# Strassen's seven products for 36 of the 66 pairs of gate and up tiles, in three feed-forward layers

## The reference, cut to what matters

```python
h = rms_norm(x, g)
f = (jax.nn.silu(h @ w_gate) * (h @ w_up)) @ w_down
x = x + f            # normed first in gen 1, times 0.5 in gen 2 and 5
```

## Time and profile before

| | |
|---|---|
| median of 3 runs | 1947.0 us (1946.43 to 1948.33) |
| profiled execution | 1947.51 us, span of its instructions 1945.8 us |
| PE busy, matmuls | 1924.7 us (99% of the span), 9634 instructions |
| DVE, ACT, POOL busy | 999.6, 753.3 and 240.1 us |
| PE's share of the chain that ended last | 93% |
| HBM | 90 GB/s over the span |

### The profile page before, as it was taken

How to read it: one execution, slowest core, us unless ns; L and a number is a source line. 1 busy time by engine, 2 the same in 40 slices (tenths; PEclk the granted TensorE clock), 3 DMA queues, 4 the chain that set the end, 5 groups by cost and what they waited for, 6 DMA issues and landing times.

```text
span 1945.8 us, 23922 instructions
## 1 busy us (share of the span) xinstructions
PE 1924.7 (99%) x9634; PEld 1564.1 (80%) x9634; DVE 999.6 (51%) x1497; ACT 753.3 (39%) x1165; POOL 240.1 (12%) x240
## 2 busy tenths in 40 slices
PE   9999999999999999999999999999999999999998
PEld 7777788878888888788888888777787788888887
DVE  6677535373334345733333367887654444333335
ACT  6344534453223233432322256665543333233224
POOL 5210001201011011010100112222010011011010
PEclk9999999999999999999999999999999999999999
DMA  6222233433333323333333232222332233333323
GB/s 174 58 65 66 59 99 103 119 98 98 98 97 98 98 85 111 97 95 96 95 96 97 81 113 66 66 66 66 87 98 65 76 97 96 95 96 96 97 59 104
DMA packets 340767, 176.32 MB, mean 91 GB/s; under 512 B 6481, under 2 KB 339378, under 8 KB 340658
## 3 DMA queue, kind: packets, MB, share of 16 engines
q1 hardware_dynamic: 340658, 174.79, 30.7%
HBM read 172.67 MB, written 2.10 MB: 90 GB/s over the span
## 4 chain that ended last, share of the span: by engine, by line
PE 93%; DVE 3%; ACT 2%; DMA 1%; issue 1%; POOL 0%; SPq 0%; ACTq 0%; DVEq 0%
PE ps L1107 28%; PE ps L1109 28%; PE ps L1111 28%; PE ps L1167 1%; PE ps L1147 1%; PE ps L1156 1%; PE ps L1252 1%; PE ps L1120 1%; PE ps L1270 1%; PE ps L1130 1%; PE ps L1181 1%; PE ps L1137 0%; DVE WL L1562 0%; DMA RAW<-in_ffn_w_down 0%; ACT WH L1313 0%
## 5 line engine op out<-in xcount | busy, mean ns | idle before, releaser
L1107 PE MATMUL ps<-HH,WH 128*128 128x512 f32 x1728 | 687.8, 398 | 1.3 <-ACT HH L1323 1.3
L1111 PE MATMUL ps<-HL,WH 128*128 128x512 f32 x1728 | 673.9, 390 | 0.8 <-DVE HL L1583 0.8
L1562 DVE TENSOR_TENSOR WL<-RAW,WH 128x1024 fp32r<-128x1024 f32 (+3 forms) x335 | 400.8, 1199 | 532.5 <-ACT WH L1313 532.0
L1109 PE MATMUL ps<-HH,WL 128*128 128x512 f32 x1728 | 673.2, 390 | 0.7 <-DVE WL L1562 0.7
L1313 ACT ACTIVATE WH<-RAW 128x1024 fp32r<-128x1024 f32 (+3 forms) x335 | 337.6, 1010 | 520.2 <-PE ps L1111 516.7
L1107 PEld LDWEIGHTS ps<-HH,WH 128*128 128x128 f32 x1728 | 324.4, 188 | 78.1 <-issue 9.7
L1109 PEld LDWEIGHTS ps<-HH,WL 128*128 128x128 f32 x1728 | 324.5, 188 | 72.1 <-issue 5.5
L1111 PEld LDWEIGHTS ps<-HL,WH 128*128 128x128 f32 x1728 | 324.3, 188 | 71.5 <-DVE HL L1583 2.1
L1107 PE MATMUL ps<-GH,WH 128*128 128x512 f32 x688 | 269.2, 391 | 0.0
L1111 PE MATMUL ps<-GL,WH 128*128 128x512 f32 x688 | 267.9, 389 | 0.0
L1109 PE MATMUL ps<-GH,WL 128*128 128x512 f32 x688 | 267.8, 389 | 0.0
(11 more groups left out here) (202 smaller groups left out, 1526.8 us busy)
## 6 DMA issues: line engine op xcount, KB each, us to landing
RAW<-in_ffn_w_gu SPq DMA_DIRECT2D x88, 512.0 KB, 3.8
RAW<-in_w_in SPq DMA_DIRECT2D x67, 512.0 KB, 3.8
RAW<-in_ffn_w_down SPq DMA_DIRECT2D x32, 512.0 KB, 4.1
RAW<-in_w_gate SPq DMA_DIRECT2D x22, 512.0 KB, 3.8
RAW<-in_w_up SPq DMA_DIRECT2D x22, 512.0 KB, 3.8
RAW<-in_w_out SPq DMA_DIRECT2D x16, 512.0 KB, 4.2
RAW<-in_mem_w_kv SPq DMA_DIRECT2D x16, 512.0 KB, 4.0
RAW<-in_w_down SPq DMA_DIRECT2D x16, 512.0 KB, 3.9
```

The source lines that it names most:

```text
L1107: e.matmul(bk, wh, xh, start=k == 0, stop=False)
L1109: e.matmul(bk, wl, xh, start=False, stop=False)
L1111: last = e.matmul(bk, wh, xl, start=False, stop=k == kt - 1)
L1562: e.tensor_tensor(at.weight(n, "L"), m["RAW"][:, n % NRAW, 0:kt, :], at.weight(n, "H").bitcast(F32), ALU.subtract).then_inc(*sg.inc("lo", n))
```

## The change

In each layer the first five gate and up tiles (f 0 to 4) stay as they were. From then on `PAIRS` names tiles f that are taken together with f+1: f=5 in the first third, 0, 3 and 6 in the second, 0 and 3 in the last, 6 pairs a layer. The other tiles, f=7, then 2 and 5, and 2 and 5, stay plain. For a pair, the 256 x 1024 weights and the 1024 x 512 input are each seen as 2 x 2 blocks, and a gate (or up) matrix is seven products of one half weight tile (128 x 512) with one block of 4 chunks x 256 rows: 7 x 4 x 3 = 84 matmuls of 256 columns (`product`, L1338, L1340, L1342) where there were 48 of 512. Nothing else of the matmuls changes.

What it adds:

- DVE forms four sums of weight blocks per matrix (`combine_weights`, L1847) from the two RAW tiles; each is then split like a weight.
- During f 0 to 3 DVE makes the normalised input, chunk by chunk (`normal`, L1854, x2 a tile), POOL forms four sums of its blocks (`mix`, L2281 to L2286), ACT and DVE split them into NH and NL (`mix_split`, L1553, L1860). During the up tile of f=4 the normalised chunks take the place of HH and HL (`place`, L1558, L1866). The later plain tiles so need neither `normed` nor `gate_r`: silu reads PSUM (`gate_plain`, L1565).
- The seven products go into five banks. The sixth is added on top of the third's bank when ACT has copied that (L1570, event s1), the seventh on top of the second's when DVE has read that (`sum_two`, L1883 and L1886, event c22). DVE adds the partial results in 256-column instructions (L1873, L1883, L1886, L1891, L1909, and L1900 for up); POOL multiplies gate by up (`gate_mixed`, L2294).
- Masks for the mixer are written by POOL during the down tiles of gen 2, since NH and NL lie over their place.

The core of the diff:

```diff
+PAIRS = ((5,), (0, 3, 6), (0, 3))
+LOOK = 8
+MIXED = (("b", 2), ("c", 0), ("a", "11"), ("e", 1), ("d", 3), ("a", "21"), ("c", "22"))
...
+    def weigh_pair(self, key, name, c0):
+        n, r = len(self.weights), len(self.raws)
+        self.raws += [(name, 0, KD, c0 + P), (name, 0, KD, c0)]
+        self.weights += [("sum", key, 2), ("sum", key, 1), ("half", r + 1, 0), ("sum", key, 3), ("half", r, 1), ("half", r + 1, 1),
+                         ("sum", key, 4)]
...
+        self.spent += [r] * 4 + [r + 1] * 2 + [r + 2]
+        self.raw_done[r] = (("lo", n + 4), ("comb", (key, 3)))
+        self.raw_done[r + 1] = (("lo", n + 2), ("lo", n + 5), ("comb", (key, 4)))
...
     def split_to(self, n):
...
+            self.step("split", i, self.hfree)
             self.n_split += 1
...
+            while self.n_dma < min(len(known.raws), known.spent[i] + NRAW):
                 self.dma()
+            for w, need in zip(known.weights[i + 1:i + 1 + LOOK], known.needs[i + 1:i + 1 + LOOK]):
+                if w[0] == "sum" and need < self.n_dma:
+                    self.combine_to(w[1], max(w[2], self.combined.get(w[1], 0)))
...
+    def product(gen, key, i, n):
...
+        elif i == 5:
+            g.wait_ge(*sg.at("gate_act", ("s1", key)))
+        else:
+            g.wait_ge(*sg.at("part_sum", ("c22", key)))
...
+    def combine_weights(key, j):
...
+        g.wait_ge(*sg.at(f"d_raw{rb % NRAW}", rb))
+        g.wait_ge(*sg.at(f"d_raw{ra % NRAW}", ra))
```

More of the change, by code:

```diff
@@ L247, in turn, with split_tile @@
         return dst, ("td", dst)
[L249 to L250 removed]
+    def split_tile(self, src, ev, buf, gen, n, also=()):
+        self.step("split_tile", src, ev, buf, gen, n, (self.gfree if buf == "G" else self.hfree) + also)
+        if also:
+            self.tiles.give(src, ("xl", (buf, gen, n)))
     def scores(self, u, i, q, k):
@@ L369, in pipeline, with normal, mix @@
             step()
-    def ffn(self, gen, gate, g0, up, u0, down, evac, third0):
-        R = None
+    def normal(self, gen, c, gcol):
+        self.tiles.take(("N", gen, c))
+        self.step("normal", gen, c, gcol + c, self.norm(gen))
+    def mix(self, gen, c, gcol):
+        if c < 4:
+            self.normal(gen, c, gcol)
+            self.normal(gen, c + 4, gcol)
+            for a in range(2):
+                self.tiles.take(("mix", gen, c, a))
+            self.step("mix", gen, c)
+        if c:
+            for a in range(2):
+                self.step("mix_split", gen, c - 1, a, self.mixed_free)
+                self.tiles.give(("mix", gen, c - 1, a), ("op_lo", (gen, c - 1, a)))
@@ L375, in ffn @@
+    def ffn(self, gen, gate, g0, up, u0, down, evac, third0, gcol):
+        R, pending = None, []
         for n, (f0, nf) in enumerate(THIRDS):
@@ L398, in ffn @@
                 self.step("gate_r", key, go, R)
-                if not n == f == 0:
-                    mu, = self.mtiles([su], ("H", gen, 0), [bu])
-                self.step("gate_up", key, mu, bu)
+                if f == PLAIN - 1:
+                    self.mix(gen, f, gcol)
+                    self.tiles.give(("R", ("n", gen)), ("N", (gen, 7)), ("gr", key))
+                if f:
+                    mu, = self.mtiles([su], ("H", gen, 0), [bu], ahead=f < PLAIN - 1)
+                if f == PLAIN - 1:
+                    self.place(gen)
+                    self.ahead(len(self.weights))
+                self.step("gate_up", key, mu, bu, ("gr", key))
                 self.banks.give(bu, ("gu", key))
@@ L404, in ffn @@
                 self.tiles.give(("gt", key), ("xl", ("G", G, f)))
+                if f < PLAIN - 1:
+                    self.mix(gen, f, gcol)
+            while pending:
+                self.split_tile(*pending.pop(0))
             if n == 2:
-                self.end_norm(gen, ("pj", ("gt", (G, nf - 1))), ("gr", (G, nf - 1)))
+                self.hfree = self.mixed_free = (done,)
+                for half in range(2):
+                    self.held["L", half] = self.held["PT", half] = (done,)
             if n == 2 and gen == 5:
@@ L413, in ffn @@
                 evac(n, mt, b, mm)
-                self.split_to(len(self.weights) + NSPL)
+                if n == 2 and gen == 2:
+                    for i in LATE[mt]:
+                        self.step("consts", i, done)
+                self.ahead(len(self.weights))
             self.gfree = (mm,)
@@ L886, in second_block @@
         self.out_proj(5, "mem_w_o_2", 8, COL["ffn2_norm_2"], [step, None, lambda: turned(3), None, step])
+        self.mixed_free = sum((self.held[b, half] for b in ("L", "PT") for half in range(2)), ())
+        self.mixed_free += (("go", 3), ("go", 2), ("at", (3, 7)), ("dB", 3))
         self.half_ffn(5, "ffn2_w_gu_2", "ffn2_w_down_2", None, 9)
@@ new lines, in split, with mix_split, place @@
+        e.activation(at.weight(n, "H"), at.raw(n), ACT.Copy).then_inc(*sg.inc("hi", n))
+    def mix_split(gen, c, a, free):
+        g.wait_ge(*sg.at("mixed", (gen, c, 2 + a)))
+        wait_all(free)
+        e.activation(m["NH"][:, 2 * a:2 * a + 2, c, :], blocks(at.tile(("mix", gen, c, a)), 256), ACT.Copy).then_inc(*sg.inc("op_hi", (gen, c, a)))
+    def place(gen, c, free):
+        g.wait_ge(*sg.at("N", (gen, c)))
+        g.wait_ge(*sg.at(*free))
+        e.activation(m["HH"][:, c, :], at.tile(("N", gen, c)), ACT.Copy).then_inc(*sg.inc("xh", ("H", ("n", gen), c)))
```

399 lines of the change are left out of this document (335 added, 64 removed).

## The result

The changed kernel takes 2031.6 us (median of 4 runs, 2030.43 to 2034.68), the kernel before 1947.4 (4 runs on the same chip): ratio 1.0432, 95% interval 1.0419 to 1.0445. It is 84 us slower, inside the range and 25 us above the forecast of 2006. The profiled execution took 2032.34 us, its span 2030.6.

The account below looks back on a forecast made before the run. PE, busy 99% of the span, bounds the kernel: 1947.5 - 29.0 (matmuls) + 28.8 (landing waits) + 3 x (13.9 + 6) (starts, POOL) = 2007.0 us profiled, 2006.5 as median, 3.1% slower; range 1955 to 2040.

Parts of the forecast that it names:

- Matmuls: PE, 36 gate and up matrices of pairs: each falls from 10.88 to 10.08 us, 29.0 us saved in all.
- DVE inside a pair: DVE's work per pair matrix, some 9.4 us against 10.08 of PE: nearly full but covered, costed at nothing.
- the price without cover: DVE inside pairs, were its lag not covered: 36 matrices of up to 0.5 us, 18 us.
- Landing waits in the middle: Nine up matrices' seventh products: DVE's sum awaits a just-released load, PE loses 3.2 us each, 28.8 in all.
- Start of the layers: f 0 to 4: DVE's longer list and its waits make the first product late, 13.9 us a layer.
- my terms for the last NL: Layer start, DVE's list up to the last NL: 50.3 us against PE's 40.5, so 9.8 us late.
- POOL beside DVE: Layer starts, 16 mix instructions: DVE held where both read SBUF, 0 to 13.3 us, taken as 6 a layer.
- The clock: PE's clock falling in new gaps: no term in the sum, only 13 us over twelve gaps in rival 4.
- rival 4: Worse by more: ports cost 13 us a layer and PE's clock falls in the new gaps, 2041 us; chance 0.16.
- rival 1: Whole kernel: the gain comes, DVE out of PE's way, 1918 us, to 1943 if gaps mostly absorbed; chance 0.09.
- rival 2: Mid-layer: the nine landing waits alone cost time, the layer starts are covered, 1947 us; chance 0.07.
- rival 3: Layer starts alone cost time, loads land under 1 us more than PE allows, 1978 us; chance 0.08.

Follow-up runs that it names:

- run 4: The change with only pairs that have no further pair behind them in their third, 18 matrices as seven products in place of 36: 1998.1 us, ratio 1.0261.
- run 7: The change with input preparation spread over the first third's eight tiles, no pair there, and weight sums one split ahead (LOOK = 1): 1965.7 us, ratio 1.0091.
- run 9: run 7 with the place step behind the last gated tile of the first third, not ahead of it: 1946.7 us (10 runs), ratio 0.9997.
- run 1: The change with LOOK 0 in place of 8, each weight sum directly ahead of the split that reads it: 1986.7 us, ratio 1.0203.
- run 2: The change with POOL's four mix instructions made memsets of the same tiles, all waits kept, operands wrong: 2014.0 us, ratio 1.0338.
- run 3: The change with no tile taken as a pair, the preparation and place step kept: 1968.8 us, ratio 1.0113.
- run 11: run 9 with no split planned behind a pair's second and third products: 1927.0 us, ratio 0.9893.
- run 8: run 7 with 42 matrices, pairs 0, 2, 4, 6 and 0, 2, 4, without plain tiles between them: 2009.1 us, ratio 1.0311.
- run 12: run 11 with 42 matrices in place of 30, the pairs of run 8: 1974.6 us, ratio 1.0136.

## Why the prediction was right, and by how much it was off

- **Matmuls**: -29.0 forecast, -29.5 measured, 0.82 us a matrix. Right; run 4 fits it as a difference of two kernels.
- **DVE inside a pair, costed at nothing**: right for the change as a whole, where these small waits hide behind the large ones and no more than 1.4 us is left for them outside the starts and the nine places. Wrong as a statement on pairs: once the large waits were gone (runs 7 and 9) c22 was late by 0.48 us in 24 matrices, 11.4 us, of the 18 us that I had named as the price without cover. It was order, not load: two held splits removed it.
- **Landing waits in the middle**: nine, in the places named, 3.64 us each against 3.2. The mechanism is shown by run 1 (order) and run 4 (place). The error is the landing: from issue to landing these nine loads took 3.9 to 5.2 us, 4.4 in the mean, where I had taken the page's median of 3.8. The release came 0.2 us sooner than forecast in the mean (0.5 sooner in six places, 0.3 later at pair 3 of the second third), and the list behind the landing took 4.9 us, as forecast.
- **Start of the layers**: 13.9 + 6 = 19.9 a layer forecast, 19.1 of waits and 2.6 of low clock measured, 21.7. The waits come near the forecast, but in part by errors that cancel: up to the end of the first product PE waited 17.3 us, where I had 15.8, and behind it 1.8, where I had 4.1. The sums' early place cost 7.0 (run 1) and POOL's reads 5.9 (run 2), each as a difference from the whole change, so the two may overlap. The preparation alone cost 7.3 (run 3), 4.9 of it waits; my terms for the last NL without the two landings (7.6) and the seven sums (4.8) leave 9.8 + 6 - 12.4 = 3.4. So the preparation was put some 1.5 us too low, and its low clock was left out.
- **POOL beside DVE**: 6 taken of 0 to 13.3 (16 instructions at 0.87 make 14.0, a slip that changes nothing), 5.9 measured. That it is so near is luck, since the 6 were a middle between two bounds. The Trainium skill ("SBUF — State Buffer", "Who interferes with whom") says that a DVE instruction with two SBUF inputs contends with GpSimd instructions that read SBUF, not with those that only write; run 2 agrees (1.76 us beside reads, 1.22 beside memsets).
- **The clock**: this is the step that failed. The sum had no term for it, and I left it to rival 4, at 1.1 us in twelve gaps, 13 us. It cost 22.8: 15.1 in the nine middle places (1.68 each) and 7.8 at the starts (2.6 each). In the fence above PE had been idle 2.89 us and had gone on for 1.15 when the granted clock fell. The Trainium skill ("TensorE: Matmul & The Clock Gate", "What's actually happening") has the throttled state as the default that activity releases; the prediction set that rule beside the waits at the starts, and the trace shows the lower level behind each of the nine middle waits as well. Of the 25 us between forecast and result, 22.8 are the low clock and 3.9 the longer middle waits; the small pieces add 1.4, the starts' waits (-2.3) and the matmuls (-0.5) go the other way.

Of the rivals, 1 to 3 fell; the right answer was the forecast with rival 4's clock and without its ports. None named what run 11 shows: that the gain was to be had from the same arithmetic, by the place of the steps in the lists and six matrices fewer.

## What to carry to other kernels

Where engines take their work in a fixed order, put the instruction that the busiest engine waits for ahead of everything that is only early, and never behind one that waits for a load just released. Price a new gap in PE as the wait and the low clock behind it: here 3.64 us of wait cost 5.3. And when an arithmetic saving costs another engine work, look for a stretch with slack for it before looking at the saving: the same preparation cost 22 us in four tiles (run 3) and at most 4 in eight (run 11: 1927.0 us, where 30 matrices at 0.8 us would give 1923.4 if nothing else cost time).

## What was not expected of the hardware

- One wait of about 3 us in PE was enough for the clock to fall. It fell up to 1.3 us after PE had gone on, and in three of nine places before that, the earliest 2.4 us into the wait. The waits of runs 1, 8 and 12, up to 1.8 us at a time, brought no low clock in the middle of the layers.
- The port price falls on both sides, and in this trace on the one that began second. The split at 440.07 began 0.51 us into a `mix` instruction and took 1.76 us in place of 1.22, and the `mix` instruction at 440.70, begun inside that split, took 1.72 in place of 0.74. At 428.62 a split began first, kept its 1.22, and the `mix` instruction 0.22 us behind it took 1.60. The longest, in gen 2, waited behind two NL and a split, each of which kept its usual time:

```profile
866.31 1.29 DVE L1860 TENSOR_TENSOR NL<-TS,NH 128x512 fp32r<-128x512 f32 x2
867.51 1.22 DVE L1834 TENSOR_TENSOR WL<-RAW,WH 128x1024 fp32r<-128x1024 f32 x1
```

```profile
866.53 2.79 POOL L2281 TENSOR_TENSOR TS<-TS 128x256 f32<-128x256 f32 x1 [5.13 <-DVE TS L1854]
```
